# Fourteen row dots moved into the stage that chooses the experts, and the third norm's squares summed on VectorE

## The reference

```python
q = (xt @ wq).reshape(t, PEER_HEADS, 2, PEER_HALF_DIM)
sc = jnp.einsum('thpc,hpnc->thpn', q, sub_keys).astype(jnp.float32)
top_v, top_i = lax.top_k(sc, PEER_TOPK)                 # 16 of 128 keys, per half
cand_v = (top_v[:, :, 0, :, None] + top_v[:, :, 1, None, :]).reshape(t, PEER_HEADS, kk)
best_v, best_pos = lax.top_k(cand_v, PEER_TOPK)         # 16 of the pairs
gate = jax.nn.softmax(best_v, axis=-1)
...
hc = jnp.einsum('cd,chkd->chk', xc, u[ec])              # one dot of 2048 per chosen expert
ac = gc * jax.nn.gelu(hc)
return jnp.einsum('chk,chkd->cd', ac, v[ec])            # gated sum of rows of v
```

```python
h = h + peer_ffn(rmsnorm(h, ffn_norm_g[i]), ...)
gate = jax.nn.sigmoid(rmsnorm(h, ple_norm_g[i]) @ ple_w_gate[i])
h = h + gate * (p[i] @ ple_w_proj[i])
```

## Time and profile before

| | |
|---|---|
| median of three runs | 3013.22 us |
| the profiled execution | 3015.15 us |
| its span, first to last instruction | 3013.1 us |
| TensorE busy | 2955.4 us, 98% of the span |
| VectorE busy | 2463.0 us, 82% |
| ScalarE busy | 1056.8 us, 35% |
| GpSimd busy | 808.3 us, 27% |
| chain that ended last | TensorE 65%, VectorE 19%, DMA 8%, SyncE's queue 5% |

### The profile page before, as it was taken

The page is one execution under the profiler, slowest core; times in us unless marked ns, Lnnn a source line. Parts: engine busy times, 40 slices in busy tenths (PEclk is TensorE's granted clock), DMA queues, the critical chain, the costliest instruction groups (busy, mean ns, idle before and its releaser), DMA issues.

```text
span 3013.1 us, 45463 instructions
## 1 busy us (share of the span) xinstructions
PE 2955.4 (98%) x17342; PEld 2752.7 (91%) x17342; DVE 2463.0 (82%) x3640; ACT 1056.8 (35%) x1431; POOL 808.3 (27%) x535
## 2 busy tenths in 40 slices
PE   9999999999999999999999999999999999999997
PEld 7777778899989999999999999999999999999786
DVE  7544444489989969999999999999999999998644
ACT  5224432222235653333333333333333333334422
POOL 0120000036765112222222222333333343332100
PEclk9999999999999999999999999999999999999998
DMA  4243222345557689999999999999999999994322
GB/s 171 89 157 105 77 82 94 107 118 119 115 118 245 245 313 362 369 375 358 367 383 357 370 374 353 368 369 373 372 363 380 362 379 365 362 367 171 98 97 98
DMA packets 206627, 779.48 MB, mean 259 GB/s; under 512 B 50512, under 2 KB 99920, under 8 KB 132176
## 3 DMA queue, kind: packets, MB, share of 16 engines
q1 hardware_dynamic: 133920, 413.90, 37.9%
q0 software_dynamic: 67680, 358.71, 32.8%
q10 hardware_dynamic: 4944, 5.81, 0.5%
HBM read 745.22 MB, written 33.10 MB: 258 GB/s over the span
## 4 chain that ended last, share of the span: by engine, by line
PE 65%; DVE 19%; DMA 8%; SPq 5%; issue 2%; ACT 1%; DVEq 0%; ACTq 0%
PE bank L638 20%; PE bank L639 20%; PE bank L640 19%; DVE row L1948 6%; DVE w_lo L1583 5%; SPq L596 4%; DMA raw_whole<-in_u_t 3%; DMA raw_b_whole<-in_u_t 3%; DVE h L2131 2%; PE bank L729 1%; DVE w_lo L1570 1%; PE bank L752 1%; PE bank L730 1%; PE bank L932 1%; DMA raw_whole<-in_v_t 1%
## 5 line engine op out<-in xcount | busy, mean ns | idle before, releaser
L638 PE MATMUL bank<-x_hi,w_hi 128*128 128x342 f32 (+1 forms) x2880 | 1000.6, 347 | 26.2 <-DVE w_lo L1583 18.6
L639 PE MATMUL bank<-x_lo,w_hi 128*128 128x342 f32 (+1 forms) x2880 | 995.1, 346 | 0.0
L640 PE MATMUL bank<-x_hi,w_lo 128*128 128x342 f32 (+1 forms) x2880 | 988.8, 343 | 0.0
L638 PE MATMUL bank<-a_hi,w_hi 128*128 128x342 f32 x2048 | 652.9, 319 | 7.4 <-DVE a_lo L2046 4.5
L640 PE MATMUL bank<-a_hi,w_lo 128*128 128x342 f32 x2048 | 652.1, 318 | 0.0
L639 PE MATMUL bank<-a_lo,w_hi 128*128 128x342 f32 x2048 | 649.7, 317 | 0.0
L638 PEld LDWEIGHTS bank<-x_hi,w_hi 128*128 128x128 f32 x2880 | 546.6, 190 | 71.4 <-DVE w_lo L1583 21.2
L640 PEld LDWEIGHTS bank<-x_hi,w_lo 128*128 128x128 f32 x2880 | 545.6, 189 | 38.1
L639 PEld LDWEIGHTS bank<-x_lo,w_hi 128*128 128x128 f32 x2880 | 545.2, 189 | 38.2 <-issue 1.2
L638 PEld LDWEIGHTS bank<-a_hi,w_hi 128*128 128x128 f32 x2048 | 387.0, 189 | 12.0 <-issue 5.8
L639 PEld LDWEIGHTS bank<-a_lo,w_hi 128*128 128x128 f32 x2048 | 387.2, 189 | 0.0
(11 more groups left out here) (262 smaller groups left out, 3146.8 us busy)
## 6 DMA issues: line engine op xcount, KB each, us to landing
raw_whole<-in_v_t SPq DMA_DIRECT2D x62, 1024.0 KB, 8.0
raw_b_whole<-in_v_t SPq DMA_DIRECT2D x62, 1024.0 KB, 7.8
raw_b_whole<-in_u_t SPq DMA_DIRECT2D x46, 1024.0 KB, 9.8
raw_whole<-in_u_t SPq DMA_DIRECT2D x46, 1024.0 KB, 9.0
raw_whole<-in_u_t SPq DMA_DIRECT2D x72, 512.0 KB, 3.9
beside<-gate_matrix SPq DMA_DIRECT2D x31, 704.0 KB, 15.1
raw_whole<-in_w_o SPq DMA_DIRECT2D x32, 512.0 KB, 4.2
raw_whole<-in_w_q SPq DMA_DIRECT2D x32, 512.0 KB, 4.4
```

Of the source, the lines that this page charges most:

```text
L638: pe.matmul(out, w_hi[slot][:, blk, :], m_hi, start=first, stop=False)
L639: pe.matmul(out, w_hi[slot][:, blk, :], m_lo, start=False, stop=False)
L640: return pe.matmul(out, w_lo[slot][:, blk, :], m_hi, start=False, stop=last)
```

## The change

1. The first 14 dots of the 128 (all of head 0's experts: slots 0 to 13) are taken out of the expert groups and done in the choice stage, two in each pass of the loop for heads 2 to 7 and two in the eighth pass. They go through one buffer, `top_row`, for which room is made by moving `cand_cut`, `pick`, `picked`, `pos_b` and `ranks`; `stage0` moves too, because its place is that of `dots`, which is now written earlier. GpSimd gathers them between the puts, one behind the first put of a head and one behind the ninth, each after the dot before it.
2. `x_rows` is therefore made in the first pass of the choice loop (written out now, `turning=True`) and no longer behind the loop.
3. The eight early dots stay where they are, but are dots 14 to 21. Group 0 keeps 3 dots and group 1 keeps 11; groups 2 to 14 have 10 or 11 (135 in all, 149 before).
4. The first rows of group 0 are gathered all together at the later of the two points.
5. The third norm's squares are added by VectorE in `third_lo`; the last group does two chunks in each quarter instead of four, and the `w_lo` of the second unit of `p`'s projection comes behind the ninth chunk's copy, one chunk later.

```diff
+TOP = 14
 EARLY = 8
+FRONT = TOP + EARLY
...
+        top_row = at("top_row", one + 33 * K, [P, D])
...
             if g < G_DOT:
-                return 12 if g % 2 == 0 and g < 14 else 11
+                return 11 if g in (2, 5, 7, 10, 12) else 10
             return 10 if g % 3 == 1 else 11
...
+            def top_dot(k):
+
+                if isinstance(k, int) and k == 0:
+                    dve.wait_ge(rows_out, 4)
+                dve.wait_ge(top_row_in, 16 * k + 16)
+                dve.scalar_tensor_tensor(top_row[:, :], top_row[:, :], 1.0, x_rows[:, :], ALU.mult, ALU.mult,
+                                         accum_out=column(dots, k)).then_inc(row_done, 1)
...
                 query_out(2 * i, 0, u)
+                if not isinstance(i, int):
+                    top_dot(2 * i - 4)
                 half_topk(step, 2 * i - 1, 1)
                 lo(u + 3, odd)
                 best_pairs(step, mid=lo_half(u + 4, even, 0), late=lo_half(u + 4, even, 1))
                 query_out(2 * i + 1, 1, u + 2)
+                if not isinstance(i, int):
+                    top_dot(2 * i - 3)
...
+            choose_head(1)
+            dve.wait_ge(rows_out, 4)
+            with dve.Fori(2, PH) as i:
+                choose_head(i)
...
                 dve.scalar_tensor_tensor(x2_lo[:, c, :], h[:, c, :],
...
+                dve.wait_ge(h3_sq, c + 1)
+                dve.wait_ge(acc_step, ACC + c + 1)
+                dve.tensor_tensor(acc[:, :], acc[:, :], sq_h[c % 2][:, :], ALU.add).then_inc(acc_step, 1)
...
+            def load_top(k):
+
+                if k:
+                    pool.wait_ge(row_done, k)
+                pool.indirect_dma_start(top_row[:, :], None, u_rows,
+                                        bass.IndirectOffsetOnAxis(ap=expert[:, k // TOPK, k % TOPK:k % TOPK + 1], axis=0))\
+                    .then_inc(top_row_in, 16)
+
             for hd in range(PH - 1):
                 for k in range(TOPK):
                     put_gate_of(hd, k)
+                    if k in (0, TOPK // 2):
+                        load_top(2 * hd + k * 2 // TOPK)
...
-            pool.wait_ge(g_in[0], 16)
-            for k in range(EARLY, EARLY + 2):
-                load_row(k)
```

More of the change, by code:

```diff
@@ L408, in first_place @@
         def first_place(g):
-            return EARLY + sum(group_rows(j) for j in range(g))
+            return FRONT + sum(group_rows(j) for j in range(g))
         def first_a(g):
-            since, k = (0, EARLY) if g < G_DOT else (G_DOT, 0)
+            since, k = (0, FRONT) if g < G_DOT else (G_DOT, 0)
             return k + sum(len(a_places(j)) for j in range(since, g))
@@ L1322, in rows_evict, with choice @@
                 act.activation(x_rows[:, 4 * P * i:4 * P * (i + 1)], bank[6 + i % 2][:, :], ACT.Copy).then_inc(rows_out, 1)
-            act.wait_ge(zeros_stored, 16 * 2 * PUT_TB)
-            for n in range(4):
-                rows_stage(n)
+            def choice(i, turning=False):
+                u = 4 * i + U_WQ - 2
+                hi(u + 1, (U_WQ + 1) % 2)
+                score_out(2 * i - 1, 1)
+                if turning:
+                    act.wait_ge(zeros_stored, 16 * 2 * PUT_TB)
+                    for n in range(4):
+                        rows_stage(n)
+                hi(u + 2, U_WQ % 2)
+                spill(2 * i - 2, 0, u + 1)
+                if turning:
+                    rows_evict(0)
+                    rows_evict(1)
+                    for n in range(4, 8):
+                        rows_stage(n)
+                hi(u + 3, (U_WQ + 1) % 2)
+                score_out(2 * i, 0)
+                hi(u + 4, U_WQ % 2)
+                gates(i - 1)
+                spill(2 * i - 1, 1, u + 3)
+                if turning:
+                    rows_evict(2)
+                    rows_evict(3)
+            choice(1, turning=True)
+            with act.Fori(2, PH) as i:
+                choice(i)
+            score_out(2 * PH - 1, 1)
             for e in range(PLAIN):
@@ L2339, in load_row @@
             def load_row(n, index=None, table=None):
[L2341 to L2345 removed]
+                b = row_slot(n)
+                into = (early_row if n < FRONT else row)[b]
+                if n < FRONT:
+                    before = n - 2 if n >= TOP + 2 else -1
+                elif n < FRONT + 4:
                     before = -1
@@ L2354, in load_row, with load_group @@
                     .then_inc(row_in[b], 16)
-            def load_group(g, table, start=0):
-                for n in range(start, group_rows(g)):
+            def load_group(g, table):
+                for n in range(group_rows(g)):
                     if n in a_places(g):
```

133 lines of the change are left out of this document (55 added, 78 removed).

## The result

The changed kernel takes 3027.24 us in the median of nine runs (3014.80 to 3034.86), the kernel before 3008.96 us in nine runs beside it (3006.78 to 3013.69). The ratio is 1.0051, with a 95% interval from 1.0038 to 1.0064: slower by about 15 us by that ratio (the two medians lie 18 us apart), where I had forecast 2997 us, 0.5% faster, and a range of 2988 to 3012 us. The profiled execution took 3030.38 us, with a span of 3028.5 us.

The account below looks back on a forecast made before the run. VectorE's overlong queue was taken to bound the dot stage, TensorE the mix stage. Choice +20, gate and group 0 +0.5, dots -34.2, third norm -2.5 gave -16.2 us: 2997 us, range 2988 to 3012 us.

Parts of the forecast that it names:

- The step that failed: Choice stage: GpSimd stays inside the pass, with two gathers of some 1.6 us on top of 27 us busy.
- The rival of late rows: Choice stage: gathered rows land late and VectorE waits, deciding from a 9.9 us landing; 3020 or 3050 us; chance 0.10.
- row waits: Choice stage: VectorE waits for the first gathered row in seven heads, +3 us, with bounds of 0 and 26 us.
- the two cases that stood for it: Whole kernel: the forecast, 2989 to 3006 us, chance 0.66; and the choice stage's shift partly hidden, 2990 us, chance 0.12.
- Dots and `x_rows`: Choice stage: fourteen dots cost 15.9 us after filling old waits, and making `x_rows` in the first pass costs 1 us.
- The gate stage and group 0: Gate stage and group 0: gathers collide with weight loads at a later time, +0.5 us (-2 to +4).
- The dot stage: Groups 2 to 14: fewer dots make TensorE the bound at 52.49 us a group, -34.2 us.
- The third norm: End of the kernel: VectorE's adds bring the first copy of a `proj` bank earlier, -2.5 us (-4 to +1).
- the sum's four terms: Whole kernel: choice stage +20, gate stage and group 0 +0.5, dot stage -34.2, third norm -2.5, together -16.2 us.

Follow-up runs that it names:

- early_gather: Changed kernel with each head's first gather issued behind the previous head's last put and the second behind put 5: ratio 0.9985 to the kernel before.
- no_gather: Changed kernel with its fourteen top dots but thirteen of the fourteen gathers left out: ratio 1.0006 to the kernel before.
- norm_only: Kernel before with only the third norm changed as in the change: ratio 1.0014 to the kernel before.
- seven: Changed kernel with one top dot a head instead of two, and the third norm's adds back on GpSimd: ratio 0.9951 to the kernel before.
- seven_proj: The kernel seven with the third norm's adds on VectorE and ScalarE's first three proj copies moved earlier: ratio 0.9946 to the kernel before.
- proj_early: Changed kernel with ScalarE's first three proj copies placed between its third_hi steps, adds still on VectorE: ratio 1.0022 to the kernel before.
- half_gather: Changed kernel with thirteen of fourteen gathers bringing 4 KB a row instead of 8 KB: ratio 0.9999 to the kernel before.
- few_puts: Changed kernel with only the even eight of sixteen puts for heads 0 to 6: ratio 1.0022 to the kernel before.

## Why the prediction was wrong

**The step that failed** is "GpSimd itself stays inside the pass: two gathers of some 1.6 us on top of 137.28 / 5 = 27 us busy". Busy time was the wrong measure for a queue. In the kernel before the puts of a head hold GpSimd for 35.1 us: 28 busy, 0.30 between two of them, and a stall of 2.75. Against that stood a pass of 41.6 us. The two gathers take 2.6 us with their gaps, the stall grows by 2.7, and the two puts that now run beside dots (3.20 and 3.45 us for 1.55) bring 3.6: 44.1 us in the worst head. The 35.1 us and the gathers stood in the trace of before. Their sum of 37.7 us is what the first two heads measure (37.5 and 37.9 us), and it still fits, with 3.9 us to spare. The longer puts and the doubled stall took that rest in two heads of seven; they couldn't be read from before, and should have been a bound. They moved the second gathers too: forecast for 20.5 us behind the `cell`, these went out at 22.5 to 23.9 us, and one at 26.4. The cost is 311.0 - 288.4 = 22.6 us, shown by early_gather, which changes nothing but the order on GpSimd. It is made up of 20.8 us less of VectorE's waits for rows and weights, and 1.8 us less of its busy time.

**The rival of late rows** named the right place and the wrong mechanism. It tied the price to the landing of a gather, from 9.9 us on (by its own rows from 10.2 - 3.25 + 2.7 = 9.65 us). The slowest took 9.5 us, and the kernel was slower all the same, because the time between `cell` and issue grew from 3.25 to 6.3 and 6.5 us in two heads. With 3 us of my sum given to row waits and a bound of 26, the 14.6 us lay inside the bound. The 7.1 us of new waits for weights I had not counted; early_gather has 0.9 us of them, but 3 us stand in no_gather too, where no row is late. What I should have done with a chance of 0.10 is ask for every cause that makes a row late, not for one. The chances don't quite add up either: 0.75 for faster is less than the 0.66 and 0.12 of the two cases that stood for it.

**Dots and `x_rows`** were right: 15.9 + 1 = 16.9 us forecast; in early_gather 15.1 us from the first to the eighth `cell`, and 1.0 us ahead of the first, where `x_rows` is now made.

**The gate stage and group 0** came to +2.6 us up to the end of group 1, for +0.5, inside my -2 to +4.

**The dot stage** was right in mechanism and too large in size: -29.7 us for -34.2. The wait for `w_lo` fell to 2.0 us, under the 4 I had named, and the clock rose to 1.00. In nine executions with 135 rows the stage takes 683.7 to 689.2 us, so 682.4, my 13 x 52.49, is a floor and not a mean. And the kernel before scatters: norm_only, which is alike in this stage, took 711.2 us where the profiled execution took 716.6; the medians of the kernel before beside the experiments are 3008.7 to 3011.8 us, under that execution's 3015.15. Part of the gain I counted may have been one execution's bad luck. The shortfall of seven would fit that too, and the 700.6 us of seven_proj; this is argued and not shown.

**The third norm** had its sign wrong: +3.6 us for -2.5. The step followed VectorE's queue alone ("the first copy of a `proj` bank comes earlier"). TensorE needs a copy from each engine in turn, and ScalarE's came 7.6 us later, behind twelve pairs where it had stood behind eight. proj_early shows that the -2.5 was there to be had (269.9 us for 273.1, in one execution each).

Of the sum's four terms, then, 18.4 us were lost in the first, 2 in the second, 4.5 in the third and 6 in the fourth, and the result is 15.4 us above before in place of 16.2 below.

## What to carry to other kernels

Measure a queue by the time from its first to its last instruction in a period, gaps and stalls included, and set that against the period; a busy share of 70% can be a queue with hardly any time left (27 busy of 38.7 us, and 35.1 held). Look at every period, not at the mean: here two heads of seven ran over by 1.75 us. Where it can, a prefetch is issued ahead of the wait that its engine stands in, not behind it; that is one of the two moves that gave 20 us back here. When work moves to another engine, read the queue of every engine that paces it or is paced by it, since a copy that nobody moved can end up behind the slower one.

## What the runs showed of the hardware

- An instruction on GpSimd's DMA queue can stand, waiting for nothing that the profile names, until an earlier gather has landed, and starts 0.39 us after that: 4.65 to 5.48 us behind gathers of 1 MB in the changed kernel, 1.85 to 2.49 us behind the same ones with 512 KB. In each of the four executions with the changed kernel's choice stage it happens behind the 6th, 9th and 12th gather alone (3.39 to 5.89 us). It is not gathers alone: with puts only, the kernel before has nine stalls of 1.8 to 2.8 us, six of them fifteen puts apart and three 28 puts apart. So the place in the row of requests matters; what sets it is open. The Trainium skill, "DMA: Bandwidth & Descriptors", section "SWDGE vs HWDGE vs iDMA", says that GpSimd writes the descriptors of its DMAs into rings in SBUF, with a single queue. No run here shows a ring, and that a full one is the cause is a guess. In early_gather, with the same requests in another order, no stall is above 1.4 us.
- A put takes 1.54 us in most cases. Puts that overlap a dot of 2048 elements on VectorE take 1.54 to 3.45 us in the changed kernel, eight of them over 3 us; the longest are those that overlap it for 2.0 us.
- The landing of a gather of 128 rows, in the median: 4.9 us with 4 KB a row (half_gather); with 8 KB 5.6 us in early_gather, 6.0 in few_puts and 7.7 in the changed kernel. The fit in "DMA: Bandwidth & Descriptors" of the Trainium skill, section "Anatomy of one DMA — SWDGE (gpsimd) path", gives an estimate of 3.2 and 4.4 us; the traces are 1.7 us above it for 4 KB, and 1.2 to 3.3 us above it for 8 KB.
